# The same instructions at other places: a new order of the tensors in on-chip memory

## The reference, cut to what matters

```
x = layer_norm(ALPHA * x + h, ...)                       # h: differential, then dilated attention
x = layer_norm(ALPHA * x + memory_cross_attention(...), ...)
x = layer_norm(ALPHA * x + conv_glu(x, w_in, conv_w, conv_b, w_out), ...)
...
h_lat = h_lat + g1 * y_lat                               # ssd_mixer, then conformer_conv_module
h_lat = h_lat + g2 * swiglu(modulate(rmsnorm(h_lat, g), sh2, s2), ffn_w_in, ffn_w_out)
return rmsnorm(h_lat, final_norm_g)
```

## Time and profile before

| | |
|---|---|
| median of three runs | 2019.91 us (2018.1 to 2021.36) |
| the profiled execution | 2021.36 us, the slowest of the three |
| its span, first to last instruction | 2019.2 us |
| busy PE, PEld, POOL, DVE, ACT | 1901.2, 1690.0, 1249.4, 1077.0, 996.4 us |
| read from main memory | 339.65 MB |

### The profile page before, as it was taken

How to read it: one execution, slowest core, us unless ns; L and a number is a source line. 1 busy time by engine, 2 the same in 40 slices (tenths; PEclk the granted TensorE clock), 3 DMA queues, 4 the chain that set the end, 5 groups by cost and what they waited for, 6 DMA issues and landing times.

```text
span 2019.2 us, 33951 instructions
## 1 busy us (share of the span) xinstructions
PE 1901.2 (94%) x13633; PEld 1690.0 (84%) x13633; DVE 1077.0 (53%) x1502; ACT 996.4 (49%) x1703; POOL 1249.4 (62%) x585
## 2 busy tenths in 40 slices
PE   7989999999999989999998899999889999989997
PEld 7879798887999866879978787877679988959996
DVE  5472246633610172145556655688449943947971
ACT  4654345543444463436653454578645535535542
POOL 8758466787888504559895343100669886218885
PEclk9999999999999999999999899999999999989999
DMA  7435378864555534445552222344345554225552
GB/s 265 145 129 206 109 283 305 317 259 175 198 188 188 204 131 168 166 163 191 189 196 100 69 99 84 125 147 167 127 151 184 184 183 156 89 86 174 187 188 104
DMA packets 49218, 342.32 MB, mean 170 GB/s; under 512 B 5264, under 2 KB 7312, under 8 KB 8144
## 3 DMA queue, kind: packets, MB, share of 16 engines
q1 hardware_dynamic: 47440, 331.02, 45.5%
q0 software_dynamic: 1664, 9.70, 1.2%
HBM read 339.65 MB, written 1.05 MB: 169 GB/s over the span
## 4 chain that ended last, share of the span: by engine, by line
PE 71%; DVE 10%; POOL 8%; ACT 5%; issue 4%; DMA 0%; DVEq 0%; POOLq 0%; SPq 0%; ACTq 0%
PE bank L1831 12%; PE bank L1768 11%; PE bank L1771 11%; PE bank L1774 11%; POOL w_lo L2339 7%; PE bank L1881 3%; PE bank L1806 2%; PE bank L1809 2%; PE bank L1811 2%; PE bank L1353 2%; PE bank L1356 2%; PE bank L1355 2%; PE bank L1587 2%; DVE arena L765 2%; ACT arena L1181 1%
## 5 line engine op out<-in xcount | busy, mean ns | idle before, releaser
L2339 POOL TENSOR_TENSOR w_lo<-ring,w_hi 128x1024 fp32r<-128x1024 f32 x404 | 979.2, 2450 | 298.5 <-ACT w_hi L2949 280.9
L1768 PE MATMUL bank<-x_hi,w_hi 128*128 128x256 f32 x2176 | 615.3, 283 | 18.1 <-POOL w_lo L2339 13.6
L1774 PE MATMUL bank<-x_lo,w_hi 128*128 128x256 f32 x2176 | 611.5, 281 | 0.0
L2949 ACT ACTIVATE w_hi<-ring 128x1024 fp32r<-128x1024 f32 x448 | 448.7, 1051 | 284.6 <-DMA ring<-slabs_dram 277.9
L1771 PE MATMUL bank<-x_hi,w_lo 128*128 128x256 f32 x1824 | 513.7, 282 | 0.0
L1768 PEld LDWEIGHTS bank<-x_hi,w_hi 128*128 128x128 f32 x2176 | 418.8, 192 | 29.0 <-issue 28.3
L1774 PEld LDWEIGHTS bank<-x_lo,w_hi 128*128 128x128 f32 x2176 | 414.4, 190 | 0.0
L1771 PEld LDWEIGHTS bank<-x_hi,w_lo 128*128 128x128 f32 x1824 | 348.1, 191 | 0.0
L2871 ACT ACTIVATE arena<-bank 128x512 f32<-128x512 f32 (+1 forms) x179 | 98.6, 563 | 278.3 <-PE bank L1774 194.8
L458 POOL TENSOR_TENSOR w_lo<-ring,w_half 128x1024 fp32r<-128x1024 f32 x32 | 76.8, 2407 | 111.3 <-ACT w_half L1069 111.3
L2339 POOL TENSOR_TENSOR w_hi<-ring,w_hi 128x1024 fp32r<-128x1024 f32 x44 | 104.4, 2394 | 44.9 <-ACT w_hi L2949 44.9
(11 more groups left out here) (365 smaller groups left out, 3655.6 us busy)
## 6 DMA issues: line engine op xcount, KB each, us to landing
ring<-slabs_dram SPq DMA_DIRECT2D x308, 1024.0 KB, 4.8
lnrow<-ln_dram POOLq DMA_DIRECT2D x6, 1024.0 KB, 6.6
arena<-slabs_dram SPq DMA_DIRECT2D x4, 1024.0 KB, 8.4
xt<-xT_dram SPq DMA_DIRECT2D x1, 1024.0 KB, 5.8
xt<-memT_dram SPq DMA_DIRECT2D x1, 1024.0 KB, 12.0
x<-x_dram SPq DMA_DIRECT2D x1, 1024.0 KB, 13.7
arena<-ctx_dram POOLq DMA_DIRECT2D x1, 1024.0 KB, 7.0
lnrow<-ln_dram POOLq DMA_DIRECT2D x2, 512.0 KB, 4.7
```

Of the source, the lines that this page charges most:

```text
L1768: ins = pe.matmul(dst, wh[:, k, c], src[0][:, k, :], start=(k == 0 and (ch == 0 or not both)), stop=False, skip_group_check=both)
L1774: ins = pe.matmul(dst, wh[:, k, c], src[1][:, k, :], start=False, stop=(k == KC - 1), skip_group_check=both)
L2339: pool.tensor_tensor(dst[:, c], ring[:, s, c], w_hi[:, s, c].bitcast(F32), ALU.subtract).then_inc(S["lo_ready"], 1)
L2949: a.activation(w_hi[:, g % RING, c], ring[:, g % RING, c], ACT.Copy) \
```

## The change

The tensors are allocated in another order, and a few places inside them are redrawn. `xt2` comes directly behind `x`; `tri` before `lnrow`; `small` goes from the end to behind `row`; `arena` is last and 16 words shorter. `w_hi` starts at word 20,480 of the arena instead of 20,496. In `small`, which is 16 words longer, `dcol` has columns of its own (it shared those of `nmx`), and `pick`, `lamp` and `dtn` start 24 words later. By the same sizes the places after are: ring 16,512; x 49,280; xt2 57,472; tri and x_lo 80,512; small 102,336; xlat 106,432; arena 114,624; x_hi 188,352; w_hi 196,544, ending at 229,312.

```diff
         ring = sb("ring", [P, RING, SLAB])
         x = sb("x", [P, NT, D])
+        xt2_at = aligned()
+        xt2 = sb("xt2", [P, KC, 2 * T])
+        xT = xt2[:, :, T:2 * T]
+        sideT = xt2[:, :, 0:T]
         ident = sb("ident", [P, P])
         dist0 = sb("dist0", [P, 2 * T])
         dist_at = aligned()
         dist = sb("dist", [P, NT, 2 * T])
+        tri_at = aligned()
+        tri = sb("tri", [P, 4, NT, T])
         lnrow = sb("lnrow", [P, 2, D])
+        pt = sb("pt", [P, NPT])
         row = sb("row", [P, NROW])
+        small = sb("small", [P, 544])
         mod = sb("mod", [P, 2, 6, 8, 2])
         sc_in = sb("sc_in", [P, KC * 32 + 30])
         xlat = sb("xlat", [P, KC, T])
-        pt = sb("pt", [P, NPT])
-        tri_at = aligned()
-        tri = sb("tri", [P, 4, NT, T])
-        xt2_at = aligned()
-        xt2 = sb("xt2", [P, KC, 2 * T])
         arena_at = aligned()
-        arena = sb("arena", [P, 28688])
-        small = sb("small", [P, 528])
-        xT = xt2[:, :, T:2 * T]
-        sideT = xt2[:, :, 0:T]
+        arena = sb("arena", [P, 28672])
...
-        pick = small[:, 232:264]
+        pick = small[:, 256:288]
         modA = small[:, 168:184]
-        lamp = small[:, 264:392]
-        dtn = small[:, 264:520].rearrange("p (t h) -> p t h", t=4)
+        lamp = small[:, 288:416]
+        dtn = small[:, 288:544].rearrange("p (t h) -> p t h", t=4)
...
-        dcol = small[:, 56:72]
+        dcol = small[:, 232:248]
...
-        w_hi = part("w_hi", arena_at + 4 * 20496, RING, SLAB)
+        w_hi = part("w_hi", arena_at + 4 * 20480, RING, SLAB)
```

## The result

The changed kernel takes 2034.4 us (median of four runs, 2033.2 to 2035.6), the kernel before 2019.0 us in the same comparison (2012.9 to 2021.4). The ratio is 1.0081, with a 95% interval of 1.0057 to 1.0104: slower by 0.8%, some 15 us. The forecast was 2019.9 us, at most 2031. Over all experiments the kernel before ran on several chips with medians of 2012.6, 2016.2 and 2018.2 us and a spread of 11.5 to 14 us in each; the changed one spreads over 2.3 in its four runs. That was the first hint: the time before is a lottery, and the time after is not.

What follows compares the result with a forecast made beforehand. TensorE's steady matmul pace was taken to bound the kernel; all five parts were costed at 0, so the forecast stayed at the median, 2019.9 us. Likeliest case 2016 to 2024 us (0.53); 8 in 10 range 2008 to 2031.

Steps and rivals of the forecast that it cites:

- What bounds the kernel: Whole span: TensorE, busy 94%; the end moves with its pace, its clock, or a feeding engine slowed beyond its slack.
- Does an address set the pace?: Matmul stretches at 113 and 117.5 ns: both paces at fixed addresses, so a phase of TensorE, not an address conflict; 0 taken.
- Part 1: Moved matmul operands (w_hi, x_hi, x_lo, xt2): 0 taken, bounds -16.3 and +13.9 us if addresses choose the pace.
- Rival B: Narrow stretches (network from 900 us, two head groups, pointwise stage) go wide: 10.7 us slower, 2030.6 us; 0.20 with partial forms.
- Part 2: Converters, ScalarE writing w_hi and GpSimd's subtraction at L2339: move costs 0, with 3.5 us allowed either way.
- part 4: Columns inside small (dcol, pick, lamp, dtn): no wait hangs on the sharing, so 0.
- part 5: Transfers to moved places: 0 taken; 1.6 us if each of 16 or so moved by 0.1 us in the open.
- Part 3: VectorE beside GpSimd on the shared port pair: they wait as whole instructions, the same ones meet after the change, so 0.
- Rival D: Matmuls at a distance below both paces, 109.2 ns: 34 us off if wholly freed; unpriced in the sum, within a 0.27 chance.
- Rival E: Granted clock, 93 us at the 1.2 GHz level: 0 change, 1 to 2 us scatter; inside the 0.53 no-effect case.
- A: Wide pace gives way in the two late networks: 9.1 us off, 2010.8 us; 0.27 with partial forms and a smaller distance.

Runs made afterwards that it cites:

- the map: Matmul streams alone on TensorE, operands at chosen places: one pair 0, 64, 128, 192 bytes apart modulo 256 took 120.00, 113.33, 118.57, 117.78 ns.
- the moved ring: Against the kernel before, row allocated ahead of ring and sc_in behind it, putting ring and w_lo at 0 modulo 256: 2016.35 us, ratio 0.9987.
- the mended order: Changed kernel's order with pt and row ahead of xt2 and tri; w_hi, w_lo, x_hi, x_lo at 0, 128, 192, 192 modulo 256: 2018.5 us, 0.9999 to before.

## Why the prediction was wrong

- **What bounds the kernel** was right: TensorE's pace moved, and the end with it; no other engine's time did.
- **"Does an address set the pace?" is the step that failed.** I saw both paces at the same addresses and concluded that the address does not choose, so I took 0. The observation was right and the inference was not. The places set which phases exist and which are stable; the way in picks one of those. Before's places have two, and so show both paces at the same addresses. The changed places of these four have one, 115.55 ns, wherever slab follows slab. That it is the places is shown from both sides: with the changed residues and little moved the loss is there (1.0085), with before's residues and the operands far away it is not (1.0007). Equal addresses with unequal pace exclude an address as the only cause. They do not exclude it as one.
- **Part 1's bounds** were built from the two paces that the trace showed, and only for the 256-column stretches counted in the earlier trace rows: at most +13.9 us. The result is +15.4. L1806 to L1811 got a pace, 120.0, outside both; L1831 and the mixer, which I did not price, gave 3.4 and 1.4 us of the 12.5.
- **Rival B** named the right direction and a wrong mechanism. It had the narrow stretches turn wide, +10.7 us; in fact narrow and wide alike went to 115.55, so h0 and h1 gained 2.2 us each while f1 lost 2.3.
- **Part 2** (converters) held in the means, by 0.5% and 0.1%, as did part 4 as far as anything shows; **part 5** was not isolated. **Part 3** said that by the Trainium skill (SBUF — State Buffer, "Who interferes with whom") the layout is worth nothing. The page lists for TensorE two independent read ports and says that PE never waits on anyone. The stream alone, with nothing else at work, takes 113.33 to 120.0 ns by the distance of its two operands: here the measurement decides, and that TensorE's two reads are independent in time does not hold for these matmuls. Its rule between engines isn't touched by a stream of TensorE alone.
- **Rival D** quoted 109.2 ns for 256 columns from the Trainium skill (TensorE: Matmul & The Clock Gate, "Back-to-back issue gap"). No combination of places here went below 113.33 over a stream; the page's figure is for matmuls by themselves, these alternate with weight loads.
- **Rival E** took the clock at 0 with 1 to 2 us of scatter; it was 3.5 us in the pair of traces, with 15.4 us more at half speed.
- The sign chosen for the larger rival, A over B, rested on counting which matmuls could gain. Before's distance of 64 bytes was already the best of the four in the map, so the expectation for a blind move should have leaned to slower.

## What to carry to other kernels

When a stream of matmuls fills the span, look at the distance from start to start, and where two values stand side by side for the same instruction, treat the places of its operands as a parameter. Put the weight and the activation at chosen distances on a 256-byte grid, measure the stream alone for all combinations (one short kernel did 64), then check in the whole kernel that the narrow pace is stable, not only possible. And keep the residues when tensors are re-ordered: here 64 bytes in one tensor cost 1.5%. A kernel whose repeats spread by 0.5% while a variant's spread by 0.1% may be telling of a choice between phases. Here that is argued: each kernel left one trace, so no two repeats of before were compared stage by stage.

## What the runs showed of the hardware, unexpected

- 256-column matmuls with a weight load each come at 113.33, 115.56, 117.78 or 120.00 ns in the steady state of most combinations. At 2.4 GHz three of them take 816, 832, 848 or 864 cycles, steps of 16 over 3 x 256: as if reads were waited for in units of 16 cycles. That reading is argued from the numbers, not shown, and the map also has steady streams off these steps, at 116.67 and 118.89 ns (840 and 856 cycles).
- The distance of the two operands counts modulo 256 bytes: 0 is the worst of the four multiples of 64 (120.0 ns), 64 the best (113.33).
- For some places two phases are stable. For before's places a passage between orders flips or keeps them by rule: flip from L1806's order to L1768's, keep the other way, in eleven passages of eleven.
- What remains open: why a stream of before's places goes wide after one pause of eight, whether `sc_in` alone decides the pace in f0 (the moved ring and the mended order have the same distances, 64, 192 and 64, at other residues), whether the phases make the whole of before's spread, and what part the half-speed intervals play.
